# The first up quad of a feed-forward layer: four whole blocks, or seven half-depth products

## The reference, cut to what matters

```python
f = rms_norm(h, ffn_pre_norm)                        # 1024 x 1024
f = (silu(f @ w_gate) * (f @ w_up)) @ w_down         # w_gate, w_up: 1024 x 2816
h = h + rms_norm(f, ffn_post_norm)
```

## Time and profile before

| what | us |
|---|---|
| median of 3 runs | 1806.12 (1805.7 to 1806.37) |
| the profiled execution | 1806.25 |
| its span, first to last instruction | 1804.1 |
| PE busy | 1790.7 (99%) |
| DVE busy | 1393.3 (77%) |
| POOL busy | 1082.5 (60%) |
| ACT busy | 700.5 (39%) |

### The profile page before, as it was taken

One profiled execution on the slowest core, in us unless ns is written; L12 is line 12 of the kernel. 1 busy time (PEld: TensorE's weight loads), 2 busy tenths in 40 slices (PEclk: granted clock), 3 DMA queues, 4 the chain that ended last, 5 costly groups with the idle time before them and its releaser, 6 DMA issues.

```text
span 1804.1 us, 22619 instructions
## 1 busy us (share of the span) xinstructions
PE 1790.7 (99%) x8518; PEld 1500.6 (83%) x8518; DVE 1393.3 (77%) x1624; ACT 700.5 (39%) x1229; POOL 1082.5 (60%) x766
## 2 busy tenths in 40 slices
PE   9999999999999999999999999999999999999998
PEld 9888888888888888888888888888888888888886
DVE  7889866656676658676599989668888875798897
ACT  6545577843421111111243334416433343333314
POOL 4066632260377879888778878632755465567554
PEclk9999999999999999999999999999999999999999
DMA  7342410032321323233375631113232241943122
GB/s 209 97 151 56 135 25 17 19 128 94 125 75 59 117 82 117 76 135 117 105 280 175 233 129 47 47 47 135 99 117 105 106 140 70 367 169 107 72 103 93
DMA packets 126974, 206.54 MB, mean 114 GB/s; under 512 B 32129, under 2 KB 88065, under 8 KB 123153
## 3 DMA queue, kind: packets, MB, share of 16 engines
q1 hardware_dynamic: 126690, 205.03, 33.5%
q10 hardware_dynamic: 176, 0.07, 0.0%
HBM read 151.51 MB, written 53.04 MB: 113 GB/s over the span
## 4 chain that ended last, share of the span: by engine, by line
PE 76%; DVE 3%; issue 1%; ACT 0%; DVEq 0%
PE ps L1362 66%; PE ps L1714 2%; PE ps L1716 2%; PE ps L1715 2%; PE ps L1953 1%; PE ps L1954 1%; PE ps L1952 1%; PE ps L1855 0%; PE ps L1829 0%; PE ps L1617 0%; PE ps L1701 0%; DVE ln_dev L3531 0%; PE ps L1590 0%; DVE hid L3309 0%; DVE y L3538 0%
## 5 line engine op out<-in xcount | busy, mean ns | idle before, releaser
L1362 PE MATMUL ps<-f_hi,ring_hi 128*128 128x512 f32 x384 | 149.6, 390 | 0.2 <-POOL ring_lo L1218 0.2
L1362 PE MATMUL ps<-f_hi,ring_lo 128*128 128x512 f32 x384 | 149.4, 389 | 0.0
L1362 PE MATMUL ps<-f_lo,ring_hi 128*128 128x512 f32 x384 | 149.4, 389 | 0.0
L2396 ACT ACTIVATE f_copy<-ps 128x512 f32<-128x512 f32 x60 | 35.8, 598 | 229.4 <-PE ps L1362 229.4
L1296 POOL TENSOR_TENSOR ring_lo<-w_sum,ring_hi 128x512 fp32r<-128x512 f32 x60 | 93.7, 1573 | 51.4 <-ACT ring_hi L2523 51.3
L1362 PE MATMUL ps<-d_w_hi,d_hid_hi 128*128 128x512 f32 x312 | 121.5, 390 | 0.3 <-DVE hid L3309 0.3
L1362 PE MATMUL ps<-d_w_lo,d_hid_hi 128*128 128x512 f32 x312 | 121.4, 389 | 0.0
L1362 PE MATMUL ps<-d_w_hi,d_hid_lo 128*128 128x512 f32 x312 | 121.4, 389 | 0.0
L1218 POOL TENSOR_TENSOR ring_lo<-w_sum,ring_hi 128x512 fp32r<-128x512 f32 x80 | 116.6, 1457 | 6.7
L1362 PE MATMUL ps<-f_low,ring_hi 128*128 128x512 f32 x320 | 111.5, 389 | 0.0
L1362 PE MATMUL ps<-xs_hi,ring_hi 128*128 128x512 f32 x256 | 99.8, 390 | 0.0
(11 more groups left out here) (565 smaller groups left out, 5903.3 us busy)
## 6 DMA issues: line engine op xcount, KB each, us to landing
d_raw<-hid_rows SPq DMA_DIRECT2D x37, 512.0 KB, 4.4
stage<-in_w_up SPq DMA_DIRECT2D x22, 512.0 KB, 4.7
wd_raw<-in_w_down SPq DMA_DIRECT2D x22, 512.0 KB, 5.2
raw_w<-in_w_gate SPq DMA_DIRECT2D x20, 512.0 KB, 5.0
stage<-in_pool_w_in SPq DMA_DIRECT2D x16, 512.0 KB, 4.8
raw_w<-in_pool_w_in SPq DMA_DIRECT2D x16, 512.0 KB, 4.7
m_rows<-u_row SPq DMA_DIRECT2D x16, 512.0 KB, 2.6
z_rows<-z_buf SPq DMA_DIRECT2D x8, 1024.0 KB, 4.1
```

What stands on the lines that cost most here:

```text
L1362: last = mm(out_ap, l, r, start=(start and j == 0), stop=(stop and j == n - 1), skip_group_check=onto)
L2396: f(copies[:, j, :], ps[:, bank0 + bank_of[o], :], ACT.Copy).then_inc(prod_copied, 1)
```

## The change

The first up quad becomes quad 0 of the products, with its seven products in the order 0, 4, 2, 1, 5, 3, 6; the gate quad stays whole. PE does gate blocks 0, 1 and 2, product 0, gate block 3, and the other six products. Its seven weight blocks go to ring slots 4, 5, 6, 7 (products 0, 4, 2, 1) and 0, 1, 2 (products 5, 3, 6; these held the gate's weights, so POOL waits there for the fourth gate block). The later quads' numbers move up by one. The second gate quad's blocks are split in the order 3, 0, 1, 2, 4, 5, 6.

The input sums are made in whole 128x2048 instructions, with the weight sums of the first up quad behind the first of them, and the low parts of `f_sum[0]` and `f_sum[1]` ahead of the weight sums of the next gate quad; the low part of `f_sum[3]` comes behind these. POOL makes the low part of `f_sum[2]` behind the seven blocks of the first up quad, and counts it on a semaphore of its own, `fs_third`. ACT's silus of the gate blocks, its high parts and its copies are put in one order. `f_raw[3]` moves to another place in SBUF, and two semaphores for square roots are merged in one.

```diff
 # PE
-            whole_quad(0, 0, (0, 1, 2, 3), True)
-            pe.wait_ge(w_split, IN_BLOCKS + 8)
-            whole_quad(4, 4, (2, 3, 0, 1), False)
+            gate_block(0)
+            f_transposed(TB - 1)
+            gate_block(1)
+            pe.wait_ge(mix_taken, TB)
+            pe.wait_ge(rows_split, 16 + 2 * TB)
+            gate_block(2)
+            quad(0, 4, factors, (0,))
+            gate_block(3)
+            quad(0, 4, factors, FIRST_ORDER[1:], ffn_sums, at=1)
             pe.wait_ge(silu_ready, 4)
-            quad(0, 0, factors, sums=ffn_sums)
+            quad(1, 0, factors, (0, 1, 2), at=1)
+            quad(1, 0, factors, (3,), at=3)
+            quad(1, 0, factors, (4, 5, 6), at=4)
             pe.wait_ge(hid_ready, 4)
-            quad(1, 4, factors)
+            pe.wait_ge(quad_summed, IN_SUMS + 4)
+            quad(2, 4, factors)
...
             def ffn_sums(o):
-                if o in (1, 2, 3, 6):
-                    pe.wait_ge(fs_split, US_PARTS + {1: 2, 2: 3, 3: 3, 6: 4}[o])
+                if o == 3:
+                    pe.wait_ge(fs_third, 1)
+                if o in (1, 2, 6):
+                    pe.wait_ge(fs_split, US_PARTS + {2: 1, 1: 2, 6: 3}[o])
 # POOL
-            whole_blocks(1, 4)
...
-            pool.wait_ge(fs_hi_ready, US_PARTS + 12)
-            g.tensor_tensor(f_sum[2][1][:], f_raw[2][:], f_sum[2][0][:].bitcast(F32), ALU.subtract).then_inc(fs_split, 1)
-            product_blocks(2, 0, std_slots_free)
+            for o in FIRST_ORDER:
+                if o in SUM_OF:
+                    pool.wait_ge(w_summed, IN_SUMS + SUM_OF[o] + 1)
+                if o == 5:
+                    pool.wait_ge(std_full, 4)
+                split_block(ring_slot(0, o), block_source(1, 1, o))
+            def second_blocks(part):
+                for o in part:
+                    if o in SUM_OF:
+                        pool.wait_ge(w_summed, IN_SUMS + 4 + SUM_OF[o] + 1)
+                    if o < 3:
+                        pool.wait_ge(prod_full, IN_BLOCKS + quad_full(0, (5, 3, 6)[o]))
+                    split_block(o, block_source(2, 0, o))
+            pool.wait_ge(fs_hi_ready, US_PARTS + 3)
+            g.tensor_tensor(f_sum[2][1][:], f_raw[2][:], f_sum[2][0][:].bitcast(F32), ALU.subtract).then_inc(fs_third, 1)
+            pool.wait_ge(raw_in[1], IN_LANDED + raw_landed(2))
+            second_blocks(SECOND_BLOCKS)
 # ACT (f_sum_hi(i, n): one 128x2048 copy into f_sum[i][0], behind n sums; silu_block(k): silu of gate block k)
-            for k in range(4):
-                for i, at_raw in ((1, 3), (0, 3), (2, 4)):
-                    act.wait_ge(fs_raw, US_SUMS + 4 * k + at_raw)
-                    f(f_sum[i][0][:, k, :], f_raw[i][:, k, :], ACT.Copy).then_inc(fs_hi_ready, 1)
-                act.wait_ge(std_full, k + 1)
-                f(silu_g[:, k, :], ps[:, k, :], ACT.Silu).then_inc(silu_ready, 1)
+            f_sum_hi(0, 1)
+            silu_block(0)
+            silu_block(1)
+            f_sum_hi(1, 3)
+            silu_block(2)
+            copy_product(0, 4, f_copy, 0)
+            silu_block(3)
+            f_sum_hi(2, 4)
+            f_sum_hi(3, 4)
+            copy_product(0, 4, f_copy, 1)
+            copy_product(0, 4, f_copy, 2)
 # DVE (f_low(i, n): low part of f_sum[i], behind n high parts)
-            for k in range(4):
-                f_sums(k)
+            s0, s1, s2, s3 = (f_raw[i][:] for i in range(4))
+            v.tensor_tensor(s0, s2, s0, ALU.subtract).then_inc(fs_raw, 1)
+            weight_sums(1, 1)
+            v.tensor_tensor(s2, s1, s2, ALU.subtract).then_inc(fs_raw, 1)
+            v.tensor_tensor(s1, s1, s0, ALU.subtract).then_inc(fs_raw, 1)
+            f_low(0, 1)
+            v.tensor_tensor(s3, f_last[:], s1, ALU.subtract).then_inc(fs_raw, 1)
+            f_low(1, 2)
             weight_sums(2, 0)
-            for i in (1, 0):
-                v.tensor_tensor(f_sum[i][1][:], f_raw[i][:], f_sum[i][0][:].bitcast(F32), ALU.subtract).then_inc(fs_split, 1)
-            weight_sums(3, 1)
...
+            f_low(3, 4)
 # SP
-            sp.wait_ge(w_split, IN_BLOCKS + 8)
+            sp.wait_ge(w_split, IN_BLOCKS + blocks_split(0) + 7)
             load_raw(0, raw_cols(0, w_up, 256))
```

More of the change, by code:

```diff
@@ L477, in wcols @@
             return w_hi[s][:, c:c + P], w_lo[s][:, c:c + P]
-        N_QUADS = 2 * FG - 2
+        N_QUADS = 2 * FG - 1
         POOL_QUADS = 16
@@ L486, in quad_full @@
         def quad_full(q, o):
+            if q == 0:
+                return FIRST_ORDER.index(o) + 1
             if q == N_QUADS:
@@ L495, in blocks_split, with ring_slot @@
         def blocks_split(q):
-            return 8 + 7 * q + (N_DOWN if q >= N_QUADS else 0)
+            return 4 + 7 * q + (N_DOWN if q >= N_QUADS else 0)
+        FIRST_SLOT = {0: 4, 4: 5, 2: 6, 1: 7, 5: 0, 3: 1, 6: 2}
+        SECOND_BLOCKS = (3, 0, 1, 2, 4, 5, 6)
+        def ring_slot(q, o):
+            return FIRST_SLOT[o] if q == 0 else o
         PHASE = (1, 3, 2, 0)
@@ L514, in build @@
         LAST_PAIR = 7 * (PAIRS - 1)
-        DOWN_W = 7 * N_QUADS + 8
+        DOWN_W = 7 * N_QUADS + 4
         ADDS = 4 * (N_DOWN + 2)
@@ L1737, in pe_program, with gate_block @@
                 f_transposed(t - 1)
[L1740 to L1755, removed]
+            def gate_block(b):
+                c, n = b % 2, b // 2
+                terms = []
+                for k in range(KD):
+                    w_h, w_l = ring[2 * c + k // 4]
+                    f_h, f_l = f_part[k // 4][n]
+                    cs = slice((k % 4) * P, (k % 4 + 1) * P)
+                    terms.append((w_h[:, cs], w_l[:, cs], f_h[:, k % 4, :], f_l[:, k % 4, :]))
+                three(ps[:, b, :], terms).then_inc(std_full, 1)
             factors = (f_part[0][0], f_sum[1], f_sum[0], f_sum[2], f_part[1][0], f_part[1][1], f_sum[3])
@@ L1779, in pe_program @@
             pe.wait_ge(mix_taken, TB - 1)
-            whole_quad(0, 0, (0, 1, 2, 3), True)
-            pe.wait_ge(w_split, IN_BLOCKS + 8)
-            whole_quad(4, 4, (2, 3, 0, 1), False)
+            gate_block(0)
[7 more added lines that the diff above has]
+            quad(0, 4, factors, FIRST_ORDER[1:], ffn_sums, at=1)
             pe.wait_ge(silu_ready, 4)
-            quad(0, 0, factors, sums=ffn_sums)
+            quad(1, 0, factors, (0, 1, 2), at=1)
+            quad(1, 0, factors, (3,), at=3)
+            quad(1, 0, factors, (4, 5, 6), at=4)
             pe.wait_ge(hid_ready, 4)
-            quad(1, 4, factors)
+            pe.wait_ge(quad_summed, IN_SUMS + 4)
+            quad(2, 4, factors)
             for g in range(2, FG):
                 pe.wait_ge(silu_ready, 4 * g)
-                pe.wait_ge(quad_summed, IN_SUMS + 8 * g - 12)
-                quad(2 * g - 2, 0, factors)
+                pe.wait_ge(quad_summed, IN_SUMS + 8 * g - 8)
+                quad(2 * g - 1, 0, factors)
                 pe.wait_ge(hid_ready, 4 * g)
-                pe.wait_ge(quad_summed, IN_SUMS + 8 * g - 8)
-                quad(2 * g - 1, 4, factors)
+                pe.wait_ge(quad_summed, IN_SUMS + 8 * g - 4)
+                quad(2 * g, 4, factors)
             def down_blocks(s, hid_s, w_s, i):
@@ L2371, in act_program @@
                                   accum_out=stat_a[:, t:t + 1]))
-                f(stat_b[:, t:t + 1], stat_a[:, t:t + 1], ACT.Sqrt, bias=EPS, scale=1.0 / D).then_inc(sd1_ready, 1)
+                f(stat_b[:, t:t + 1], stat_a[:, t:t + 1], ACT.Sqrt, bias=EPS, scale=1.0 / D).then_inc(roots_ready, 1)
                 act.wait_ge(h1_ready, t + 1)
@@ L2376, in act_program @@
                 act_own.do(act, f(f_blk[:], h1_blk[:], ACT.Square, accum_out=stat_c[:, t:t + 1]))
-                f(stat_d[:, t:t + 1], stat_c[:, t:t + 1], ACT.Sqrt, bias=EPS, scale=1.0 / D).then_inc(sd2_ready, 1)
+                f(stat_d[:, t:t + 1], stat_c[:, t:t + 1], ACT.Sqrt, bias=EPS, scale=1.0 / D).then_inc(roots_ready, 1)
                 if t >= 1:
@@ L2380, in act_program, with f_sum_hi, silu_block @@
             take_f(TB - 1)
-            for k in range(4):
-                for i, at_raw in ((1, 3), (0, 3), (2, 4)):
-                    act.wait_ge(fs_raw, US_SUMS + 4 * k + at_raw)
-                    f(f_sum[i][0][:, k, :], f_raw[i][:, k, :], ACT.Copy).then_inc(fs_hi_ready, 1)
+            def f_sum_hi(i, at_raw):
+                act.wait_ge(fs_raw, US_SUMS + at_raw)
+                f(f_sum[i][0][:], f_raw[i][:], ACT.Copy).then_inc(fs_hi_ready, 1)
+            def silu_block(k):
                 act.wait_ge(std_full, k + 1)
                 f(silu_g[:, k, :], ps[:, k, :], ACT.Silu).then_inc(silu_ready, 1)
-            act.wait_ge(fs_raw, US_SUMS + 16)
-            act.wait_ge(std_full, 6)
-            f(f_sum[3][0][:], f_raw[3][:], ACT.Copy).then_inc(fs_hi_ready, 1)
+            f_sum_hi(0, 1)
[3 more added lines that the diff above has]
+            silu_block(2)
             def copy_product(q, bank0, copies, j):
@@ L2409, in silu_quad, with gate_quad @@
```

(42 more changed lines are left out.)

27 lines of the change are left out of this document (13 added, 14 removed).

## The result

The changed kernel takes 1812.24 us (median of 7 runs, 1811.94 to 1813.02), the one before 1806.31 beside it (7 runs, 1805.7 to 1806.47). The ratio is 1.0034 [1.0024, 1.0044], so it is 5.9 us slower, beyond the 0.2% that the prediction took as what can be told apart. The forecast was 1810.3 within 1807.0 to 1813.6. The profiled execution is 1813.02 us, its span 1810.9, the slowest of the seven; by it the loss is 6.8 us.

What follows compares the result with a forecast made beforehand. PE, busy 99% of the span, was taken as the bound. −2.72 for matmuls, +5.64 and +0.12 at product 3, +0.96 and +0.12 at product 6 gave +4.12 us: 1810.3, range 1807.0 to 1813.6.

Steps and rivals of the forecast that it cites:

- rival A: PE's granted clock falls in the wait at product 3, which takes 5.44 not 2.72 us: +2.7, 1813.0; chance 0.28.
- 12 matmuls less: First up quad on PE: 84 matmuls instead of 96, at 0.2267 us each, −2.72 us.
- wait at product 3: PE waits for POOL's late low part of factor 3, in turns with DVE, until 527.4: 5.64 us, within 0 to 5.9.
- product 3 itself, restart: PE's restart after the wait at product 3 costs 0.12 us more.
- product 6 behind the copy, restart: Product 6 waits for ACT's copy of product 3 from the same bank: 0.96 us, and 0.12 for the restart.
- Products 0, 4, 2, 1, 5: no cost: These up-quad products find operands in time; the copy of product 0 has half a microsecond of margin: 0 us.
- Rival B: POOL isn't held up by DVE; its subtraction ends at 521.74, product 3 doesn't wait: −1.64, 1804.5; chance 0.12.
- rival C: POOL's subtraction gets its turn ahead of DVE's last low part: 2.15 us less, +2.0, 1808.2; chance 0.12.
- After it: no cost: After product 6, the next quad's blocks, loads and hid products are in time for PE: 0 us.

Runs made afterwards that it cites:

- experiment 2: Changed kernel, with DVE waiting for POOL's low part of factor 3 before making factor 6's: 1809.98 us, ratio 1.0021.
- experiment 3: Changed kernel, with 23 useless matmuls on PE in front of the wait at product 3: 1810.46 us, ratio 1.0023.
- experiment 4: experiment 1, with the next gate quad's product 0 put between products 3 and 6: 1811.24 us, ratio 1.0027.
- experiment 1: Changed kernel, with factor 3's low part made by DVE behind factor 1's, no longer by POOL: 1806.24 us, ratio 1.0000.
- experiment 6: experiment 1, next gate quad's blocks split 0 to 6, product 3 before 5, factor 6's low part before weight sums: 1804.04 us, ratio 0.9989.

## Why the prediction was right, and where it was off

The direction, the place and the mechanism of both waits were right, and the time lies in the range, 1.9 us above the forecast, which left the clock out. It lies outside the forecast's own range (1809.2 to 1811.4), though, and in the stated one because that took in rival A, whose 1813.0 is nearer. The terms, with what PE's starts measure:

| step | forecast | measured | from |
|---|---|---|---|
| 12 matmuls less | −2.72 | −2.72 | x8518 to x8506, at 0.2267 |
| wait at product 3 | +5.64 | +5.69 | 527.73 − 521.81 − 0.23 |
| product 3 itself, restart | +0.12 | +2.34 | 11 intervals to 532.56 in 4.83, not 2.49 |
| product 6 behind the copy, restart | +1.08 | +1.16 | 533.87 − 532.56 − 0.23, and 0.08 to 534.18 |
| sum | +4.12 | +6.47 | |

With the 0.29 us by which the stage began later, the sum is 6.76, the difference of the two spans (6.8). That last 0.29 is no step of the change (the row that starts at 492.00 in this trace, has it at 491.72, lies between 491.70 and 492.09 in the six experiments), and the medians are 5.9 apart: about 0.8 of the traced loss belongs to the one execution.

*The wait at product 3* came by the working that was given for it. POOL's last three blocks started at 511.49 and took 4.16, 2.71 and 2.72 us from start to start, and the subtraction ended at 527.59; less the 0.29 by which the stage began later that is 527.30, and the forecast had 527.3. That it is met to a tenth is in part luck: 527.3 was taken from between 527.05 and 527.6, for the part of DVE's last input sum that would be left. Strict turns with DVE are shown twice: in the changed kernel's rows, and by experiment 2, where taking one turn away gave back 2.03 us at POOL and 2.27 in PE's wait. The Trainium skill (SBUF — State Buffer, "Who interferes with whom") has the port pair that the two share as an exclusive lock, for which the order of issue decides who waits; the row of DVE at 519.85 agrees, 1.2 us ahead of POOL's.

*Products 0, 4, 2, 1, 5: no cost* held. PE has no wait between 492 and 522 us, and the copy of product 0, of which half a microsecond was said to be left, ended at 510.26 for a product at 511.16.

*Product 3 itself was the term mis-sized, and rival A the step mis-weighted.* The likeliest case left the clock out, at a chance of 0.28 for the fall; it fell, and its price, taken as 2.7 us, is 2.30 in the traces and 1.8 in the medians (experiment 3). The prediction had the row that bore on it, the tail's fall 5.2 us after its last matmul, beside a wait of 5.5 us, and still called it open, since one row can't tell whether the tail was early or late. The experiments add the rows that were lacking: the clock also falls in a wait of 3.3 us (experiment 2), and in one of 4.6 (experiment 4); with waits of 0.8 and 0.9 (experiment 1) it doesn't. With A in the sum it would have been 1813.0 by the forecast's size and 1812.1 by the size measured.

*Rival B* is refuted by POOL's end at 527.59, and *rival C* by the order of DVE's and POOL's rows. C's size, 2.15 us, is near what experiment 2 found (2.03 at POOL, 2.27 in PE's wait), but not its time: the clock fell there too, and it took 1810.0 us, not 1808.2.

*After it: no cost* held in the changed kernel, but for a reason that the step didn't name: it counted POOL's blocks against a PE that was itself about 7 us late by the forecast, and 9 in the trace. When experiment 1 took that lateness away, the blocks were late by 1.04 us, and experiment 4 ran into the same with 4.6 us. So this slack was a gift of the loss. Three of the step's sizes were off without a cost: the 6.2 us taken for a load are POOL's idle time, and the load itself was issued at 521.11 and landed by 526; the products for hid ended at 545.2, not 541; and the next gate load came 10.5 us later than before (547.07 against 536.59), not 8.

What isn't settled: the medians of experiment 6 gain 0.4 us less than −2.72 plus its traced pause of 0.2 and restart of 0.1 would give. Its trace has them nearly whole (span 1801.9 against 1804.1, the stage beginning 0.1 later), so this is within the scatter of the runs. And no run shows why the clock was back sooner in experiment 2 than in the changed kernel.

## What to carry to other kernels

Fewer matmuls on a bound engine are worth their time only if each operand of the new order is ready when it is reached; find the last producer of every factor, add up the queued turns of the engine that takes turns with it (here DVE with POOL), and give it to the engine that reaches it first. A wait on PE can cost more than itself: behind those of 3.3 to 5.5 us here the next product ran in large part at the lower clock, behind those of 0.8 and 0.9 us it didn't. After removing a wait, look again at everything that was in time only because of it, the next stage's first operands above all.

## What the runs showed of the hardware that was not expected

- The granted clock went to 0.50 in waits of 5.5, 4.6 and 3.3 us in the midst of a kernel whose PE is 99% busy, and was 1.00 throughout where 23 useless matmuls stood in the same place. The Trainium skill (TensorE: Matmul & The Clock Gate, "HAM oscillation — how this bites in real kernels") describes such a fall between bursts, and the stretches here agree.
- At the lower clock a 128x512 matmul of this kind costs 0.427 us from start to start, 1.88 times the 0.227 at the higher one, and not twice as much.
- The price of the fall was not the same each time: the 12 matmuls behind a wait of 5.5 us took 2.34 us more than on the full clock, those behind a wait of 3.3 us 1.68 more (4.17 against 2.49; a restart of 0.1 is in both), since the clock was back before the last of them.
